# The state-space branch of the second mixer as one block, with scores computed once per group

## What is computed

```python
xs = xbc[..., :GROUP_W].reshape(B_, L, H, P)
bm = repeat(B by group, H // G)          # heads 0, 1 read group 0, heads 2, 3 group 1
cm = repeat(C by group, H // G)
da = dt * (-exp(a_log))                  # one number for each token and head
cs = cumsum(da)                          # the running sum
y[l] = sum over s <= l of (C[l] . B[s]) * exp(cs[l] - cs[s]) * xs[s] * dt[s]
y = (y + xs * d_skip) * silu(z)
y = group_rms(y, M2_GROUPS) * norm_g
```

## Time and profile before

| What | us |
|---|---|
| median of 3 runs | 3285.07 (3278.49 to 3286.14) |
| profiled execution, its time | 3279.47 |
| profiled execution, its span | 3277.4 |
| PE busy in the span | 2852.3 (87%) |
| DVE, ACT busy in the span | 1667.9 (51%), 1084.0 (33%) |
| the changed branch in the span | 1872.4 to 1944.3 |

### The profile page before, as it was taken

One profiled execution on the slowest core, in us unless ns is written; L12 is line 12 of the kernel. 1 busy time (PEld: TensorE's weight loads), 2 busy tenths in 40 slices (PEclk: granted clock), 3 DMA queues, 4 the chain that ended last, 5 costly groups with the idle time before them and its releaser, 6 DMA issues. The chain is left out here.

```text
span 3277.4 us, 36751 instructions
## 1 busy us (share of the span) xinstructions
PE 2852.3 (87%) x13487; PEld 2059.1 (63%) x13531; DVE 1667.9 (51%) x2594; ACT 1084.0 (33%) x1577; POOL 154.9 (5%) x171
## 2 busy tenths in 40 slices
PE   6877778999997789999985868999989998899983
PEld 5655667888776578887774547455556655357541
DVE  4874455444554554445756543744456644157413
ACT  4343424222314242223324223222334433045301
POOL 0430000000000000000002202000000000000001
PEclk9987899999998999999995868999999999999996
DMA  3110123444321222222220004899999898999993
GB/s 124 52 52 27 64 77 116 180 156 178 113 103 65 77 77 101 80 102 78 79 90 0 1 17 179 344 401 409 404 346 359 327 408 340 405 357 351 409 397 146
DMA packets 185250, 622.10 MB, mean 190 GB/s; under 512 B 9603, under 2 KB 15394, under 8 KB 184642
## 3 DMA queue, kind: packets, MB, share of 16 engines
q1 hardware_dynamic: 170368, 568.96, 45.8%
q10 hardware_dynamic: 12322, 41.38, 3.2%
q0 software_dynamic: 2304, 8.39, 0.7%
HBM read 577.54 MB, written 41.16 MB: 189 GB/s over the span
## 5 line engine op out<-in xcount | busy, mean ns | idle before, releaser
L85 ACT ACTIVATE unit_high<-unit_whole 128x4096 fp32r<-128x4096 f32 (+2 forms) x65 | 225.6, 3471 | 446.2 <-PE psum L632 309.7
L88 DVE TENSOR_TENSOR unit_low<-unit_whole,unit_high 128x4096 fp32r<-128x4096 f32 (+2 forms) x65 | 283.3, 4358 | 175.2 <-ACT unit_high L85 174.7
L632 PE MATMUL psum<-high_parts,unit_high 128*128 128x512 f32 x640 | 254.2, 397 | 9.0 <-DVE low_parts L88 9.0
L632 PE MATMUL psum<-low_parts,unit_high 128*128 128x512 f32 x640 | 251.9, 394 | 0.0
L632 PE MATMUL psum<-high_parts,unit_low 128*128 128x512 f32 x640 | 251.7, 393 | 0.0
L85 ACT ACTIVATE moe_w_high<-ring_slot 128x1024 fp32r<-128x1024 f32 x208 | 215.7, 1056 | 60.7 <-PE psum L3205 59.6
L3028 PE MATMUL psum<-ring_slot,hT 128*64 128x512 f32 x1008 | 223.9, 592 | 5.8 <-DMA ring_slot<-in_moe_w_gu 5.8
L632 PE MATMUL psum<-unit_high,hidden_high 128*128 128x512 f32 x512 | 199.6, 390 | 0.0
L632 PE MATMUL psum<-unit_high,hidden_low 128*128 128x512 f32 x512 | 199.3, 389 | 0.0
L632 PE MATMUL psum<-unit_low,hidden_high 128*128 128x512 f32 x512 | 199.2, 389 | 0.0
L632 PE MATMUL psum<-unit_high,high_parts 128*128 128x512 f32 (+2 forms) x448 | 178.4, 398 | 20.8 <-DVE low_parts L88 17.0
(11 more groups left out here) (630 smaller groups left out, 5749.2 us busy)
## 6 DMA issues: line engine op xcount, KB each, us to landing
ring_slot<-in_moe_w_gu SPq DMA_DIRECT2D x102, 2048.0 KB, 16.1
unit_whole<-in_moe_w_gu SPq DMA_DIRECT2D x34, 2048.0 KB, 11.6
ring_slot<-in_moe_w_down SPq DMA_DIRECT2D x34, 2048.0 KB, 12.7
ring_last_slot<-in_moe_w_down SPq DMA_DIRECT2D x34, 2048.0 KB, 15.7
unit_whole<-in_w_up SPq DMA_DIRECT2D x16, 2048.0 KB, 7.5
unit_whole<-in_w_down SPq DMA_DIRECT2D x16, 2048.0 KB, 7.6
expert_rows<-zero_row ACTq DMA_DIRECT2D x15, 1536.0 KB, 5.3
unit_whole<-in_w_in SPq DMA_DIRECT2D x5, 2048.0 KB, 7.9
```

The source lines that it names most:

```text
L85: return act.activation(self.high, self.whole, ACT.Copy)
L88: return dve.tensor_tensor(self.low, self.whole, self.high.bitcast(F32), ALU.subtract)
L632: ins = pe.matmul(bank, a, c, start=(i == 0 and m == 0), stop=(i == len(products) - 1 and m == len(parts) - 1))
```

## The change

The three blocks of `mamba2` become one. Its parts:

- The scores are computed once per group (two heads share them), into two sets of banks: group 0 in banks 2 to 4, group 1 in banks 5 to 7.
- The running sum is spread for all four heads first, into banks 5, 6, 7 and 1, and ACT copies each to `m_cs_all` in SBUF, from where all later steps read it.
- The whole tile `hg_qfvg` is used, as two weight buffers of 4 x 512 (`arg`), which heads take by turns. Exponents, Exp and weights work in place in them.
- DVE makes only the diagonal 128x128 of each exponent (subtraction and mask in one instruction). Off the diagonal ACT subtracts, by a bias operand with the negated running sum, inside Exp. The four diagonals of a head are one Exp of 512 columns.
- The xs turns go to two banks, which ACT copies in two instructions; the eight small turns go to one bank and are copied in one.
- The sigmoid of z is taken first and DVE multiplies it by z early, so that one multiply instead of two stands behind the last save.
- SP issues the load of the skip weights only when the rate has landed; ACT waits for the rate alone.

The diff:

```diff
--- before.py
+++ after.py
@@ -2697,143 +2697,187 @@
...
-def mamba2(k, z, xbc, dt, out, w_all):
...
+def mamba2(k, z, xbc, dt, out, spare):
...
+    TURNED, SPREAD, SCORES = 0, (5, 6, 7, 1), (2, 5)
+    rate_ready, xs_turned, xs_saved, z_gate = k.act_made, k.pe_made, k.attnT_ready, k.squares
+    cs_ready, small_turned, small_saved = k.negmax_ready, k.attn_turned, k.normalised
+    spread, spread_saved, scored = k.roots, k.rstd, k.attn_ready
+    masked, decayed, weighted = k.scores_ready, k.probs_ready, k.dve_made
     with ExitStack() as ctx:
-        sig = k.sb("m2_sig", [P, 2, S], ctx=ctx)
+        gate = k.sb("m2_gate", [P, TT, 256], ctx=ctx)
...
-        dtcs = k.sb("m2_dt_cs", [P, TT, 2, 4], ctx=ctx)
+        dtcs = k.sb("m2_dt_cs", [P, 3, TT, 4], ctx=ctx)
...
+        cs_all = k.sb("m2_cs_all", [P, 4, S], ctx=ctx)
         e, cs, zero = (four[:, i, :] for i in range(3))
+        arg = [spare[:, TT * i:TT * i + TT, :] for i in range(2)]
+        B, C = (xbc[:, 2:4, :], xbc[:, 4:6, :])
...
+        def score(h, t):
+            bank = SCORES[h // 2] + (0, 1, 2, 1)[t]
+            at = 3 * P if t == 3 else 0
+            return k.psum[:, bank, at:at + S - t * P]
...
+        def out_bank(h):
+            return k.psum[:, h % 2, 0:TT * 64]
...
         with k.block() as block:
             @block.gpsimd
             def _(pool):
...
             @block.sync
             def _(sp):
                 sp.dma_start(small[:, 0:1], k.ins["m2_a_log_2"][0].unsqueeze(1)).then_inc(k.small_loaded.sem, 16)
+                sp.wait_ge(k.small_loaded.sem, k.small_loaded.at(16))
                 sp.dma_start(skip[:, :], k.ins["m2_d_2"][0].partition_broadcast(P)).then_inc(k.small_loaded.sem, 16)
                 sp.wait_ge(k.small_loaded.sem, k.small_loaded.at(32))
...
             @block.tensor
             def _(pe):
...
+                def scores(g):
+                    for t in range(TT):
+                        ins = pe.matmul(score(2 * g, t), B[:, g, t * P:(t + 1) * P], C[:, g, t * P:], start=True, stop=True)
+                    ins.then_inc(scored.sem, 1)
...
+                def products(h):
+                    pe.wait_ge(weighted.sem, weighted.at(h + 1))
+                    if h == 0:
+                        pe.wait_ge(small_saved.sem, small_saved.at(1))
+                    elif h == 1:
+                        pe.wait_ge(spread_saved.sem, spread_saved.at(4))
+                    else:
                         pe.wait_ge(k.out_saved.sem, k.out_saved.at(h - 1))
                     for t in range(TT):
                         for s in range(t + 1):
...
+                            ins = pe.matmul(out_bank(h)[:, t * 64:(t + 1) * 64], arg[h % 2][:, s, (t - s) * P:(t - s + 1) * P],
+                                            xd[:, s, h * 64:(h + 1) * 64], start=(s == 0), stop=(s == t))
                     ins.then_inc(k.out_ready.sem, 1)
...
+                for t in range(TT):
+                    for c in range(2):
+                        at = (t % 2) * 256 + c * P
+                        ins = pe.transpose(k.psum[:, t // 2, at:at + P], xbc[:, c, t * P:(t + 1) * P], k.ident[:, :])
+                    if t % 2 == 1:
+                        ins.then_inc(xs_turned.sem, 1)
+                scores(0)
+                pe.wait_ge(cs_ready.sem, cs_ready.at(1))
+                pe.wait_ge(xs_saved.sem, xs_saved.at(2))
+                for i, a in enumerate((dt, cs)):
+                    for t in range(TT):
+                        at = (i * TT + t) * 4
+                        ins = pe.transpose(k.psum[:, TURNED, at:at + 4], a[:, t * P:(t + 1) * P], k.ident[0:4, 0:4])
+                ins.then_inc(small_turned.sem, 1)
+                for h in range(4):
+                    pe.matmul(k.psum[:, SPREAD[h], :], sel[:, h, :], cs, start=True, stop=True).then_inc(spread.sem, 1)
+                products(0)
+                pe.wait_ge(spread_saved.sem, spread_saved.at(3))
+                scores(1)
+                for h in range(1, 4):
+                    products(h)
...
             @block.vector
             def _(dve):
+                step = lambda ins: k.dve.step(dve, ins)
...
+                def exponents(h):
+                    if h == 0:
+                        dve.wait_ge(k.pool_made.sem, k.pool_made.at(1))
+                    if h >= 2:
+                        dve.wait_ge(k.out_ready.sem, k.out_ready.at(h - 1))
+                    dve.wait_ge(spread_saved.sem, spread_saved.at(h + 1))
+                    for s in range(TT):
+                        ins = dve.scalar_tensor_tensor(out=arg[h % 2][:, s, 0:P], in0=cs_all[:, h, s * P:(s + 1) * P],
+                                                       scalar=dtcs[:, 1, s, h:h + 1], in1=later[:, :], op0=ALU.subtract,
+                                                       op1=ALU.add)
+                    ins.then_inc(masked.sem, 1)
...
+                def weights(h):
+                    dve.wait_ge(scored.sem, scored.at(h // 2 + 1))
+                    dve.wait_ge(decayed.sem, decayed.at(h + 1))
+                    for s in range(TT):
+                        w = arg[h % 2][:, s, 0:S - s * P]
+                        ins = dve.tensor_tensor(w, w, score(h, s), ALU.mult)
+                    ins.then_inc(weighted.sem, 1)
...
+                def save(h):
+                    dve.wait_ge(k.out_ready.sem, k.out_ready.at(h + 1))
+                    cols = slice(h * 64, (h + 1) * 64)
+                    y = out_bank(h).rearrange("p (t e) -> p t e", t=TT)
+                    dve.scalar_tensor_tensor(out=out[:, :, cols], in0=xs[:, :, cols], scalar=skip[:, h:h + 1], in1=y,
+                                             op0=ALU.mult, op1=ALU.add).then_inc(k.out_saved.sem, 1)
...
+                dve.memset(zero, 0.0)
+                step(dve.tensor_copy(sel[:, :, :], k.ident[0:4, 0:4].unsqueeze(2).broadcast_to([4, 4, P])))
+                dve.wait_ge(rate_ready.sem, rate_ready.at(1))
+                step(dve.tensor_scalar(e, dt, small[:, 1:2], -1.0, ALU.mult, ALU.mult))
+                dve.tensor_tensor_scan(cs, e, zero, 0.0, ALU.add, ALU.add).then_inc(cs_ready.sem, 1)
+                dve.wait_ge(z_gate.sem, z_gate.at(1))
+                step(dve.tensor_tensor(gate[:, :, :], gate[:, :, :], z, ALU.mult))
+                dve.wait_ge(small_turned.sem, small_turned.at(1))
+                dve.tensor_copy(dtcs[:, 0:2, :, :], k.psum[:, TURNED, 0:32].rearrange("p (i t h) -> p i t h", i=2, t=TT))\
+                   .then_inc(small_saved.sem, 1)
+                dve.wait_ge(small_saved.sem, small_saved.at(1))
+                dve.tensor_scalar(dtcs[:, 2, :, :], dtcs[:, 1, :, :], -1.0, None, ALU.mult).then_inc(small_saved.sem, 1)
+                exponents(0)
+                exponents(1)
+                dve.wait_ge(xs_saved.sem, xs_saved.at(2))
                 for h in range(4):
                     cols = slice(h * 64, (h + 1) * 64)
                     ins = dve.tensor_tensor(xd[:, :, cols], xs[:, :, cols],
...
+                                            dtcs[:, 0, :, h:h + 1].broadcast_to([P, TT, 64]), ALU.mult)
+                step(ins)
+                weights(0)
+                weights(1)
+                dve.wait_ge(k.small_loaded.sem, k.small_loaded.at(32))
+                exponents(2)
+                save(0)
+                weights(2)
+                exponents(3)
+                save(1)
+                weights(3)
+                save(2)
                 save(3)
...
                 dve.wait_ge(k.out_saved.sem, k.out_saved.at(4))
-                k.dve.step(dve, dve.tensor_tensor(out, out, z, ALU.mult))
...
-                k.dve.step(dve, dve.tensor_tensor(out, out, sig[:, 0:2, :].rearrange("p a (b e) -> p (a b) e", b=2),
...
+                step(dve.tensor_tensor(out, out, gate[:, :, :], ALU.mult))
...
             @block.scalar
             def _(act):
...
+                act.activation(gate[:, :, :], z, ACT.Sigmoid).then_inc(z_gate.sem, 1)
+                act.wait_ge(k.small_loaded.sem, k.small_loaded.at(16))
+                act.activation(small[:, 1:2], small[:, 0:1], ACT.Exp).then_inc(rate_ready.sem, 1)
+                for half in range(2):
+                    act.wait_ge(xs_turned.sem, xs_turned.at(half + 1))
+                    act.activation(xs[:, 2 * half:2 * half + 2, :], k.psum[:, half, :].rearrange("p (t e) -> p t e", t=2),
+                                   ACT.Copy).then_inc(xs_saved.sem, 1)
+                for h in range(4):
+                    act.wait_ge(spread.sem, spread.at(h + 1))
+                    act.activation(cs_all[:, h, :], k.psum[:, SPREAD[h], :], ACT.Copy).then_inc(spread_saved.sem, 1)
+                act.wait_ge(spread_saved.sem, spread_saved.at(4))
+                act.wait_ge(small_saved.sem, small_saved.at(2))
+                for h in range(4):
+                    act.wait_ge(masked.sem, masked.at(h + 1))
+                    diagonal = arg[h % 2][:, :, 0:P]
```

(35 more changed lines are left out.)

67 lines of the change are left out of this document (7 added, 60 removed).

## The result

The changed kernel takes 3235.15 us (median, 3232.95 to 3235.95) where the kernel of before takes 3283.86 (3278.49 to 3286.14): ratio 0.9854, 95% interval 0.9842 to 0.9867, a gain of 48.7 us. The prediction was 3250 with a range of 3242 to 3259, a gain of 32. The profiled executions are 3279.47 us before and 3235.95 after, with spans of 3277.4 and 3234.2.

A forecast was written before the change was run, and what follows sets the result against it. The prediction took the branch as a chain of waits with no engine full. Its steps summed to 34.3 us saved, 33.5 after handovers and 32 net after the projection's clock: 3250 us, range 3242 to 3259.

The forecast's parts named there:

- The failed step: Behind the changed branch: everything moves by the same amount, and the experts' stretch keeps its 1187 us within 5.
- A gain over 36 us: Whole kernel: an early clock rise saves 1.0 us in the head, 3 in scores and last products; chance 0.01.
- The branch: The edited stage, 71.9 us before: would end at 1910.0 instead of 1944.3 us, 34.3 us sooner.
- Rival 3: Head of the branch: each table load has a drain, small transposes 2.0 us late; gain 30, 3252 us; chance 0.03.
- PE is the later one by 0.6: Head of the branch: PE is free at 1878.6 us, the running sum ready at 1878.0, so an earlier rate gains nothing.
- Scores of group 1: PE, after head 0's products: from 1892.4 to 1896.0 us, 3.0 at the low clock and the rest high.
- The tail: End of the branch: head 3's products 4.5 us, save 0.5, one multiply of 1.23 instead of two.
- The 0.8 us for handovers: Across the branch: twenty handovers of some 0.05 us each, lowering the gain from 34.3 to 33.5 us.
- The 1.5 us off for the projection: Output projection behind the branch: a later clock rise could cost up to 3.3 us; 1.5 taken off the gain.
- Rival 1: Clock stays low in the branch and rises late in the projection: gain 24 us, 3258 us; chance 0.07.
- Rival 4: Experts' weight stream meets PE work less well: slower beyond 2.7% growth, 3297 us at 4%; chances 0.02 slower, 0.02 within.
- Rival 2: Branch: two weight buffers bring nothing because heads still go in turn; gain 17 us, 3265 us; chance 0.05.

The follow-up runs named there:

- after_hidden60: The changed kernel with 60 more PE instructions, already met waits hidden where PE waits for ACT in the mixer's first branch: 3245.2 us.
- before_hidden188: The kernel of before with 188 more PE instructions, already met waits hidden where PE waits for ACT in the mixer's first branch: 3266.2 us, ratio 0.9941.
- one_buffer: The changed kernel with one weight buffer instead of two, so each head's exponents wait for the products of the head before: 3247.9 us.
- before_shift50: The kernel of before with 50 more PE instructions, already met waits placed behind the branch, not hidden: 3279.4 us.
- scores_per_head: The changed kernel with scores computed for each head again instead of once per group: 3259.2 us.

## Why the prediction was right and wrong

**The failed step** is "Everything after moves by the same amount, and the experts' stretch keeps its 1187 us within 5". The stretch lost 10.2 us, and 11.3 with the projection. I looked for ways in which the stream could suffer from an earlier start, and held the code behind the change for the same because its lines were the same. What had changed was where it lies. The term put at nothing is the branch into the full expert's code behind the jump back: 14.9 us over three places before, 0.7 after. Shifts that are hidden under a wait show what the place is worth: 10 us lost on the new branch (after_hidden60), 18.7 gained on the old (before_hidden188). The evidence was in the trace of before: three idles of 9.4 to 9.6 us on PE that waited for nothing, each with code being fetched. A gain over 36 us had been given a chance of 0.01, and only by an early clock.

**The branch** was right, 34.3 forecast and 35.1 measured, in part by luck: the clock rose earlier than forecast in the head, which gave 0.8 us, and later in the scores of group 1, which took 0.8. By steps:

- The rate at +3.9 us (1876.2 of a start at 1872.4) came at +3.9, and the table loads had no drain: 1875.70 + 1.28 to 1876.99, 1878.07 + 1.28 to 1879.36. Rival 3 falls. The Trainium skill ("ScalarE: Activation LUTs", What ACT_TABLE_LOAD costs) gives 2.66 us for a switch; the trace goes against that here as it did before.
- "PE is the later one by 0.6" was wrong: the clock rose within the third microsecond of PE's work, not after seven, the scores ended early, and PE waited 1.16 us for the scan. The early clock gave more than that back: first large Exp at +10.85, forecast +11.6.
- Exponents: mean 346 ns, four in 1.14 us (forecast 1.15). Exp 1.8 a head (2.0 to 2.1), weights 1.7 (2.0). The groups after, as in the earlier trace rows:

```profile
L2810 DVE TENSOR_TENSOR hg_qfvg<-hg_qfvg,psum 128x512 f32<-128x512 f32 (+3 forms) x16 | 6.7, 482 | 5.5 <-PE psum L2750 2.8 <-ACT hg_qfvg L2873 2.7
L2873 ACT ACTIVATE hg_qfvg<-m_cs_all,m_dt_cs 128x384 f32<-128x384 f32 (+2 forms) x12 | 5.2, 492 | 0.0
L2800 DVE SCALAR_TENSOR_TENSOR hg_qfvg<-m_cs_all,m_dt_cs,m_later 128x128 f32<-128x128 f32 x16 | 4.5, 346 | 4.4 <-issue 3.0 <-ACT m_cs_all L2865 0.9 <-PE psum L2763 0.5
...
L2871 ACT ACTIVATE hg_qfvg<-hg_qfvg 128x512 f32<-128x512 f32 x4 | 2.5, 626 | 10.6 <-DVE hg_qfvg L2800 10.6
```

- Scores of group 1 took 4.4 us, not 3.6: the clock rose within 1898 to 1899, some 8.7 us after the products began; the products of head 1 then ran at the upper level (exponents of head 3 at 1901.33, forecast +26.1, measured +25.6). It fell again within 1905 to 1906, so head 3's products were low, as forecast. PE by microsecond:

```profile
1878.00:1879.00 1.00, 1.00 (x3) 0.77 0.05 2
...
1898.00:1899.00 1.00, 1.00 (x5) 0.53 0.00 0
...
1905.00:1906.00 1.00, 0.00 (x0) 0.89 0.00 0
```

- The tail: last products 4.5, save 0.5, one multiply 1.22, as forecast. The 0.8 us for handovers was not needed.

**The 1.5 us off for the projection** did not show: its clock was 0.92 over 26 us, against 0.94 in the earlier trace rows, half a microsecond.

**Rival 1** (clock low throughout) did not happen: the clock rose in both of PE's stretches. **Rival 4** had the right place and the wrong sign: the experts' stretch did change by an amount that matters, for a reason that I had not thought of. **Rival 2** fell with one_buffer.

Left open: that a fetch of PE's code is what makes a branch slow is argued from the packets, one more of which stands by every slow branch at these 39 places than by a quick one, and from the shifts, which touch PE's stream alone; no view names the engine of a packet. Where the other limits between the four classes lie is not measured. And the idles do not account for all of a profile: before_shift50, with three idles of 8 us, lies at 1317.5 us behind the projection, 6 us less than the others with such idles, and scores_per_head 6 us over before. These are single executions, and the timed runs of one kernel lie up to 10 us apart (after_hidden60, 3241.2 to 3251.8).

## What to carry to other kernels

Where code is fetched while a loop runs, as it is here, adding or removing instructions anywhere ahead of the loop can move its time by 10 to 20 us without an edit in it: look for idles with no releaser, ask for the records of the branches in front of them (here one of two had changed, and not the one that the idle suggests first), and count instruction packets there. Before a gain or a loss of that size is put down to an edit, shift the code by a few dozen instructions under cover of a wait and time it again. A chain of waits is forecast well by laying its instructions out one by one with durations from the trace; what is behind it deserves a look of its own.

## What was not expected of the hardware

- A branch of PE into a piece of code took 0.24 us or 4.7 to 5.1 us, and the jump back ahead of it 6.0 to 6.2 or 7.2 to 7.5 us, each by where the code lies. Together they left PE idle for 3.2 to 4.9 us or for 7.9 to 9.6. A shift by 32 instructions either way was enough to change the first from one to the other.
- Already met waits, two in one instruction, took PE 108 ns each (198 of them from 1912.4 to 1933.6 us).
- TensorE's clock rose within 3 us of the start of work in the new head, and only some 8.7 us after the products began, behind an idle of 4.36 us. Ahead of the projection near 990 us the same idle of 2.60 us let it fall in one execution and not in the other.
